# State-space rotations by ScalarE's sines, Toeplitz copies by parity, and MLP preloads moved later in a one-core decoder trunk

## The reference: what is computed

```python
dt = jnp.exp(log_step)[:, None]                      # 32 groups x 64 complex states
mag = jnp.exp(lam_re * dt); ang = lam_im * dt
abar_re, abar_im = mag * jnp.cos(ang), mag * jnp.sin(ang)
bb = coef * b                                        # complex, per group 64 x 16
bu = einsum('blgc,gpc->blgp', u, bb)
h[t] = abar * h[t-1] + bu[t]                         # associative scan over the tokens
y = einsum('gcp,blgp->blgc', c_re, h_re) - einsum(..., c_im, h_im) + d_skip * u
g = gelu(y); out = g * sigmoid(g @ w_glu)
```

## Time and profile before

| | us |
|---|---|
| runs | 2874.91, 2879.32, 2878.26 |
| median | 2878.26 |
| the profiled execution | 2878.83 |
| its span | 2877.1 |
| TensorE busy in it | 2715.2 (94%) |
| VectorE, GpSimd, ScalarE busy | 1487.3, 1051.8, 570.5 |

### The profile page before, as it was taken

How to read it: one execution, slowest core, us unless ns; L and a number is a source line. 1 busy time by engine, 2 the same in 40 slices (tenths; PEclk the granted TensorE clock), 3 DMA queues, 4 the chain that set the end, 5 groups by cost and what they waited for, 6 DMA issues and landing times.

```text
span 2877.1 us, 40626 instructions
## 1 busy us (share of the span) xinstructions
PE 2715.2 (94%) x16567; PEld 2580.3 (90%) x16567; DVE 1487.3 (52%) x1634; ACT 570.5 (20%) x880; POOL 1051.8 (37%) x414
## 2 busy tenths in 40 slices
PE   8979889989999999999999999977999999999997
PEld 6966579889999999999999999966989999999996
DVE  4983653714433444365667666665372344234437
ACT  4001542300000000034333443432130000000002
POOL 2532235476666666530000000010534444443542
PEclk9985799999999999999999999988999999999998
DMA  4332021352322222313111211202101111111111
GB/s 142 104 77 66 1 75 60 130 201 103 117 109 109 109 109 111 144 47 141 68 61 68 74 71 65 87 33 76 52 29 46 44 44 44 44 44 44 47 48 68
DMA packets 88993, 223.82 MB, mean 78 GB/s; under 512 B 22887, under 2 KB 38280, under 8 KB 88728
## 3 DMA queue, kind: packets, MB, share of 16 engines
q1 hardware_dynamic: 69280, 178.82, 17.8%
q10 hardware_dynamic: 19592, 43.32, 4.1%
HBM read 163.34 MB, written 58.74 MB: 77 GB/s over the span
## 4 chain that ended last, share of the span: by engine, by line
PE 63%; DVE 9%; ACT 3%; issue 2%; DMA 0%; POOL 0%; DVEq 0%; SPq 0%; ACTq 0%; POOLq 0%
PE ps L335 42%; PE ps L1708 6%; PE ps L1769 3%; PE ps L344 3%; DVE lev L1835 2%; ACT lev L1962 2%; DVE h_lo L695 2%; PE ps L415 2%; PE ps L448 1%; PE ps L462 1%; DVE ck L1835 1%; DVE ssq L673 1%; DVE cum L1835 1%; PE ps L1809 1%; DVE raw L1835 1%
## 5 line engine op out<-in xcount | busy, mean ns | idle before, releaser
L257 POOL TENSOR_TENSOR w_hi<-w_raw,ones 128x1024 fp32r<-128x1024 f32 x148 | 362.0, 2446 | 1603.1 <-PE ps L1708 653.4
L335 PE MATMUL ps<-a_hi,w_hi 128*128 128x352 f32 x1896 | 613.7, 324 | 11.7 <-POOL w_lo L259 9.3
L335 PE MATMUL ps<-a_hi,w_lo 128*128 128x352 f32 x1896 | 612.0, 323 | 0.0
L335 PE MATMUL ps<-a_lo,w_hi 128*128 128x352 f32 x1896 | 609.7, 322 | 0.0
L259 POOL TENSOR_TENSOR w_lo<-w_raw,w_hi 128x1024 fp32r<-128x1024 f32 x148 | 432.0, 2919 | 11.6
L335 PEld LDWEIGHTS ps<-a_hi,w_hi 128*128 128x128 f32 x1896 | 356.7, 188 | 13.7 <-POOL w_lo L259 5.8
L335 PEld LDWEIGHTS ps<-a_lo,w_hi 128*128 128x128 f32 x1896 | 358.6, 189 | 0.0
L335 PEld LDWEIGHTS ps<-a_hi,w_lo 128*128 128x128 f32 x1896 | 357.3, 188 | 0.0
L335 PE MATMUL ps<-h_hi,w_hi 128*128 128x352 f32 x1056 | 343.9, 326 | 6.1 <-POOL w_lo L259 6.0
L335 PE MATMUL ps<-h_hi,w_lo 128*128 128x352 f32 x1056 | 341.8, 324 | 0.0
L335 PE MATMUL ps<-h_lo,w_hi 128*128 128x352 f32 x1056 | 340.2, 322 | 0.0
(11 more groups left out here) (289 smaller groups left out, 4467.0 us busy)
## 6 DMA issues: line engine op xcount, KB each, us to landing
w_raw<-w SPq DMA_DIRECT2D x156, 512.0 KB, 3.5
p_raw<-w SPq DMA_DIRECT2D x32, 512.0 KB, 4.6
w_hi_scratch<-p_hi SPq DMA_DIRECT2D x32, 512.0 KB, 2.7
w_lo_scratch<-p_lo SPq DMA_DIRECT2D x32, 512.0 KB, 3.5
w_hi<-w_hi_scratch SPq DMA_DIRECT2D x32, 512.0 KB, 3.9
w_lo<-w_lo_scratch SPq DMA_DIRECT2D x32, 512.0 KB, 4.9
x_scratch<-x ACTq DMA_DIRECT2D x16, 528.0 KB, 2.9
x<-x_scratch ACTq DMA_DIRECT2D x16, 528.0 KB, 8.0
```

The source lines that it names most:

```text
L257: pool.tensor_tensor(hi, whole, bc(ones[:, 0:P], 1, KC), ALU.mult).then_inc(hi_made, 1)
L335: mm = pe.matmul(tiles[:, t], wt[:, b, w], at_[:, k, cols], start=(n == 0 and i == 0), stop=(n == len(ks) - 1 and i == 2))
```

## The change

1. **Rotations.** The doublings are replaced. VectorE multiplies the angle of one chunk by j (new input `jvec`, 0 to 127 on each partition, one more DMA that the first VectorE and ScalarE steps wait for), and folds the product into one turn by a rounding and a three-part subtraction. ScalarE makes sin(a/2), sin(a) and the square of the first (`act_rotations`, after `act_own_rows` and before `act_s5`); VectorE makes the cosine as 1 - 2 sin^2(a/2). Sine and cosine change places in `turn`.
2. **Toeplitz copies.** Each copy is cut in two by parity. SyncE issues all eight steps of parity 0, then steps 0 to 3 of parity 1; ScalarE issues steps 4 to 7 of parity 1. Parity 0 waits for one `lags_ready` only. The bytes are the same.
3. **Preloads.** The first MLP group has two preloads, after blocks 6 and 7; groups 1 to 6 have five each, after blocks 1, 2, 4, 5 and 7. The total stays 32.

```diff
-AHEAD_AFTER = {4: 2, 5: 2, 6: 2, 7: 2}
+AHEAD_AFTER = (1, 2, 4, 5, 7)
...
-            toep_rows(sp, range(4))
+            toep_rows(sp, 0, range(CH))
+            toep_rows(sp, 1, range(4))
             sp_k_outs(sp)
             sp_g(sp)
...
-            e = 0
             for j in range(8):
                 load(n0 + j, n0 + j, j % 2)
-                for _ in range(AHEAD_AFTER.get(j, 0)):
-                    if e == 0:
+                if j >= 6:
+                    if j == 6:
                         sp.wait_ge(x_parked, 16 * KC)
-                    ahead_in(e, e % 2)
-                    if e:
-                        ahead_out(e - 1, (e - 1) % 2)
-                    e += 1
-            with sp.Fori(1, GROUPS - 1) as g:
-                for j in range(8):
-                    load(g * 8 + (n0 + j), g * 8 + (n0 + j), j % 2)
-                    if j % 2:
-                        ahead_in(g * 4 + (4 + j // 2), (j // 2) % 2)
-                        ahead_out(g * 4 + (3 + j // 2), (j // 2 + 1) % 2)
+                    ahead_in(j - 6, j - 6)
+                    if j == 7:
+                        ahead_out(0, 0)
+            with sp.Fori(0, (GROUPS - 2) // 2) as pair:
+                e = 2
+                for half in range(2):
+                    for j in range(8):
+                        load(pair * 16 + (n0 + 8 + 8 * half + j), pair * 16 + (n0 + 8 + 8 * half + j), j % 2)
+                        if j in AHEAD_AFTER:
+                            ahead_in(pair * 10 + e, e % 2)
+                            ahead_out(pair * 10 + (e - 1), (e - 1) % 2)
+                            e += 1
...
+                        if name == "mlp0" and j >= 6:
+                            pool_ahead(pool, j - 6, j - 6, 16)
+                    if name == "mlp0":
+                        with pool.Fori(0, (GROUPS - 2) // 2) as pair:
+                            e = 2
+                            for half in range(2):
+                                for j in range(8):
+                                    block_of(pair * 2 + (1 + half), j)
+                                    if j in AHEAD_AFTER:
+                                        pool_ahead(pool, pair * 10 + e, e % 2, pair * 80 + 16 * (e // 2 + 1))
+                                        e += 1
...
-            while n < NCH:
-                wr, wi = bc(sm[:, 8], 2, n), bc(sm[:, 9], 2, n)
...
-                tt(new[0], old[0], wr, ALU.mult)
-                tt(tp, old[1], wi, ALU.mult)
-                tt(new[0], new[0], tp, ALU.subtract)
-                tt(new[1], old[0], wi, ALU.mult)
-                tt(tp, old[1], wr, ALU.mult)
-                tt(new[1], new[1], tp, ALU.add, prepared if 2 * n == NCH else None)
...
-                n *= 2
-                if n in (8, 32, 64):
-                    yield
+            half_turns, quotient = turn[:, 0], turn[:, 1]
+            tt(half_turns, bc(ang[:, CH], 2, NCH), bc(jvec[:], 1, GP), ALU.mult)
+            c.after(); c(TS(quotient, half_turns, 1 / (2 * math.pi), ROUND, ALU.mult, ALU.add))
+            c.after(); c(TS(quotient, quotient, -ROUND, None, ALU.add))
+            c.after(); c(STT(half_turns, quotient, -TWO_PI[0], half_turns, ALU.mult, ALU.add))
+            yield
+            for part in TWO_PI[1:]:
+                c.after(); c(STT(half_turns, quotient, -part, half_turns, ALU.mult, ALU.add))
+            c.after(); c(TS(half_turns, half_turns, PI_BELOW, -PI_BELOW, ALU.min, ALU.max), angles_ready)
+            yield
+            dve.wait_ge(turn_sines, 3)
+            c.after(); c(TS(turn[:, 1], turn[:, 1], -2.0, 1.0, ALU.mult, ALU.add), prepared)
...
+        def act_rotations(act):
+
+            act.wait_ge(angles_ready, 1)
+            act.activation(turn[:, 1], turn[:, 0], ACT.Sin, scale=0.5).then_inc(turn_sines, 1)
+            act.wait_ge(turn_sines, 1)
+            act.activation(turn[:, 0], turn[:, 0], ACT.Sin).then_inc(turn_sines, 1)
+            act.activation(turn[:, 1], turn[:, 1], ACT.Square).then_inc(turn_sines, 1)
...
-            pe.wait_ge(toep_in, 16 * CH)
+            pe.wait_ge(toep_in, 16 * 2 * CH)
...
-        def toep_rows(eng, steps):
+        def toep_rows(eng, par, steps):
             eng.wait_ge(toep_zero, 1)
-            eng.wait_ge(lags_ready, 2)
+            eng.wait_ge(lags_ready, par + 1)
             for s in steps:
-                eng.dma_start(toep[SC * s:SC * s + SC, :, :, SC * s:P], lags[:, :, :, 0:P - SC * s]).then_inc(toep_in, 16)
+                eng.dma_start(toep[SC * s:SC * s + SC, par, :, SC * s:P], lags[:, par, :, 0:P - SC * s]).then_inc(toep_in, 16)
```

More of the change, by code:

```diff
@@ L291, in last_group @@
                             block_of(GROUPS - 1, j, HID, spare(j - 6))
-                    e = 0
                     for j in range(8):
                         block_of(0, j, (-3, -2)[j] if j < 2 else None)
-                        for _ in range(AHEAD_AFTER.get(j, 0) if name == "mlp0" else 0):
-                            pool_ahead(pool, e, e % 2, 16 * (e // 2 + 1))
-                            e += 1
-                    with pool.Fori(1, GROUPS - 1) as g:
-                        for j in range(8):
-                            block_of(g, j)
-                            if name == "mlp0" and j % 2:
-                                pool_ahead(pool, g * 4 + (4 + j // 2), (j // 2) % 2, g * 32 + 16 * (3 + j // 4))
+                        if name == "mlp0" and j >= 6:
[9 more added lines that the diff above has]
+                                        e += 1
+                    else:
+                        with pool.Fori(1, GROUPS - 1) as g:
+                            for j in range(8):
+                                block_of(g, j)
                     last_group()
@@ L817, in build_trunk @@
         assert s1 + 9856 + 768 <= R1 + 118272
-        rest = at("rest", [P, GP * NCH // 2], s1 + 192)
-        assert 192 + GP * NCH * 2 <= 4288 + 192
+        jvec = at("jvec", [P, NCH], R1 + 116224)
         A0 = A_HI
@@ L877, in tt @@
                 c(TT_(out, a, b, op), signal)
-            dve.wait_ge(s5_in, 16 * 6)
+            dve.wait_ge(s5_in, 16 * 7)
             dve.wait_ge(dt_ready, 1)
@@ L1017, in act_prepare @@
         def act_prepare(act):
-            act.wait_ge(s5_in, 16 * 6)
+            act.wait_ge(s5_in, 16 * 7)
             act.activation(sm[:, 0], lam[:, 2], ACT.Exp).then_inc(dt_ready, 1)
@@ L1110, in quarter @@
                 i = slice(4 * q, 4 * q + 4)
-                wr, wi = turn[:, 0, i], turn[:, 1, i]
+                wr, wi = turn[:, 1, i], turn[:, 0, i]
                 vr, vi = (ps[:, 2 * (q % 2) + r].rearrange("p (i j) -> p i j", i=4) for r in range(2))
@@ L1166, in pool @@
                     i = slice(4 * q, 4 * q + 4)
-                    wr, wi, g = turn[:, 0, i], turn[:, 1, i], g_st[q % 2]
+                    wr, wi, g = turn[:, 1, i], turn[:, 0, i], g_st[q % 2]
                     hr, hi = (h_st[:, r, i, DB + 1:] for r in range(2))
@@ L1228, in act_s5 @@
                 act.activation(lags[:, par].rearrange("p (a b) n -> p a (b n)", a=4), ps[0:SC, 4:8], ACT.Copy).then_inc(lags_out, 1)
-            toep_rows(act, range(4, CH))
+            toep_rows(act, 1, range(4, CH))
             for g in range(TRIOS):
@@ L1241, in act_s5_loads @@
         def act_s5_loads(act):
-            for dst, name in ((lam, "s5_lam"), (b_in, "s5_b"), (c_in, "s5_c"), (kvec, "kvec"), (d_diag, "s5_d"), (h0, "s5_h0")):
+            for dst, name in ((lam, "s5_lam"), (b_in, "s5_b"), (c_in, "s5_c"), (kvec, "kvec"), (jvec, "jvec"), (d_diag, "s5_d"), (h0, "s5_h0")):
                 act.dma_start(dst[:], io[name]).then_inc(s5_in, 16)
@@ L2223, in _ @@
             act_own_rows(act)
+            act_rotations(act)
             act_s5(act)
@@ L2350, in layout @@
     o["kvec"] = np.broadcast_to(np.array(list(range(9)) + list(range(7, -1, -1)), np.float32), (P, 17)).copy()
+    o["jvec"] = np.broadcast_to(np.arange(SEQ // 8, dtype=np.float32), (P, SEQ // 8)).copy()
     o["ident"] = np.eye(P, dtype=np.float32)
```

15 lines of the change are left out of this document (1 added, 14 removed).

## The result

After: 2871.54 us, median of 13 runs (2858.28 to 2874.12), beside 2878.48 us for the kernel before in the same comparison (13 runs, 2874.91 to 2883.84). The ratio of the two kernels' runs is 0.9964, with a 95% interval of [0.995, 0.9977] (the two medians alone stand at 0.9976): faster, but by 0.36% where 0.6% was forecast, and outside the range of 2854 to 2868 us. Four of the 13 runs lie at 2858.28 to 2862.97, nine at 2869.83 to 2874.12. The profiled execution took 2874.12 us, with a span of 2872.3 us.

The account below looks back on a forecast made before the run. The kernel was taken as bound by a chain of waits from a weight block's DMA issued at 614.66 us. 2878.83 - 4.6 (parts 1 and 2) - 12.2 (part 3) = 2862.0, median 2861.4 us; range 2854 to 2868 us.

Parts of the forecast that it names:

- Part 1, transposes 2.5 us earlier: Rotations: v_t is evacuated earlier, so TensorE's transposes start at 166.7 instead of 169.2 us; bounds +1.8 and -5.
- the price of 0: ScalarE's rotations: Square after Sin taken to need no second table load, which would otherwise cost 1.28 us.
- Part 2, the wait for the landing turns into a wait for the states: Before the trios: earlier Toeplitz copies turn TensorE's 8 us wait for their landing into a wait for GpSimd's states.
- Parts 1 and 2, -4.6 us: Third trio, at 234.18 us before, starts at 229.5 or 230.0 us once its quarter of the states is ready.
- The trios at 0.50: TensorE's trios: idle time ahead keeps the granted clock at its lower level, the four remaining trios taking 39.0 us.
- Rival 3: The trios run at the full clock, ending 18.7 us sooner: 2843 us; chance 0.05.
- Part 3, -12.2 us: First MLP group: fewer preloads delay its weight blocks less; some 9 us are waits, the rest the clock they cost.
- Rival 4: Groups 1 to 6: the fifth preload holds up block 3; at 4 us per group 2885 us; chance 0.03.
- The later stages only move.: Whole kernel: a microsecond taken from TensorE's waits before 614.66 us comes off the end; later stages only shift.

Follow-up runs that it names:

- second profile: The changed kernel measured again, unchanged, against the kernel before: 2863.96 us, ratio 0.9931; its profile has the first lag stream at 7.16 us.
- both pauses filled: Changed kernel plus 20 unread identity matmuls on TensorE before its wait for the transposes and 8 before the lags: 2860.25 us, ratio 0.9925.
- The two later comparisons: The changed kernel measured twice more, unchanged, each against the kernel before: 2863.96 us (ratio 0.9931) and 2864.88 us (0.9941).
- reordered kernels: Changed kernel with the last rotation instruction behind v_t's evacuation and the in_ch copy: 2854.43 us; with identity matmuls before the lags 2853.23, in all pauses 2832.52.
- third profile of the changed kernel: The changed kernel measured a third time, unchanged, against the kernel before: 2864.88 us, ratio 0.9941; its profile has the first lag stream at 13.37 us.

## Why the prediction was wrong, by its own steps

- **Part 1, transposes 2.5 us earlier.** Right in direction and, in the profiles in which GpSimd's pass went first, close: 165.65 and 165.79 us against 166.7. In the others it was 163.5, by the race above, which the layout in time did not see: it took the last TENSOR_SCALAR as waiting for a GpSimd pass in any case. It also had the sines end at 163.7 us, and they ended at 160.93 us. The second table load did not come (Sin, Sin and Square took 1.92, 1.92 and 1.89 us with nothing between), so the price of 0 was right.
- **Part 2, the wait for the landing turns into a wait for the states.** Right: 0.91 us for the landing, 4.83 us for `h_st`.
- **Parts 1 and 2, -4.6 us: the step that failed.** "With the transposes 2.5 us earlier, that quarter is ready at 229.5 us" carried the lead through the lags unchanged. In the profile of the result the lag stream ran at the lower clock (13.44 for 7.16 us, and `quarter_in(0)` 3.68 for 1.97), and the mark came out at +0.96. In the same kernel's second profile the lags were fast and the mark was 228.34 us, -5.84, near the forecast 229.5. I had asked of the clock only what it does in the trios, not in the 1.97 us pause ahead of the lags, which stood in the same timeline as the earlier trace rows. What decides whether that pause costs the clock stays open; that it was the lag stream's time that ate the lead is what the profiles show. With both pauses filled the mark was 224.76.
- **The trios at 0.50.** Wrong for the first, which ran at 1.00 after its 0.91 us wait; right from the second on. It gained nothing, since the third waits for the states in either case (4.83 us). Rival 3, all trios at the full clock, came only where the waits were filled.
- **Part 3, -12.2 us.** Right in mechanism. In one pair of profiles -10.57, and nearly all of the missing 1.6 us lies in the first unit, part of it at the lower clock (15.40 for 13.85 us), which the prediction did not price; over all, the first group takes 97.3 to 101.3 us in the five profiles without part 3 and 84.4 to 86.9 in the thirteen with it, a mean of 99.5 against 86.0, -13.5. So the forecast lies between the two. Groups 1 to 6 did not grow: 93.4 to 94.6 us with four preloads and with five. Rival 4 fell.
- **"The later stages only move."** Not to the microsecond: what lies behind G took 4.46 us more in the profiled run with the same instructions, and between 2234.5 and 2244.3 us over the profiles (last section).
- The sum of 2862.0 against 2874.12 us is then: +5.6 (states, +0.96 for -4.6), +0.35 (attention), +1.6 (part 3 in this profile), +4.5 (the rest); 12.1 in all. The two later comparisons gave about the forecast change of -16.8 us (-20 and -17 by the ratios, -18 and -15 by the medians), the first did not. Run times alone can't tell whether the 13 runs there drew the slow lags more often, since the later stages scatter as much; their mean granted clocks lean to it, nine of 13.

## What to carry to other kernels

A gain in one engine's work is passed on in full only if TensorE's clock behind it stays as it was: list every pause of TensorE between the edit and the next bound, short ones too, and price the work behind each at both clocks. Look for a reorder that takes out or shortens a pause (here one instruction put behind the two that TensorE waits for, 2854 us instead of 2864 to 2872, with 1.35 us left of 4.8 to 7.2) before filling it, and fill only where no wait is added. Where two engines reach for the same moment within a few tenths of a microsecond, forecast two courses, and profile an unchanged kernel more than once before a few microseconds are explained.

## What the runs showed of the hardware

**Behind a pause of 2 us the clock may be halved for 14 to 17 us.** The same 1.97 us pause of TensorE ahead of the same 64 matmuls was followed by a stream of 7.16 us in six profiles and of 11.4 to 13.4 us in five, with the granted clock falling 0.5 to 2.6 us after work had resumed, in the middle of the busy stream. In the six profiles of the changed and reordered kernels in which fills stood in that pause, the stream took 7.16 us each time. That makes the pause the likely cause; which of its occurrences cost the clock is not settled.

**The same matmuls at the same granted clock have several paces.** VectorE's evacuations of MLP units mark 72 matmuls each. The third profile of the changed kernel, and then the first, in the second MLP:

```profile
2205.43 1.26 DVE L681 TENSOR_TENSOR ssq<-ps,rstd 128x1056 f32<-128x1056 f32 x1 [7.89 <-PE ps L343]
...
2216.87 1.26 DVE L681 TENSOR_TENSOR ssq<-ps,rstd 128x1056 f32<-128x1056 f32 x1 [4.21 <-PE ps L343]
```

```profile
2212.84 1.26 DVE L681 TENSOR_TENSOR ssq<-ps,rstd 128x1056 f32<-128x1056 f32 x1 [8.04 <-PE ps L343]
...
2224.44 1.26 DVE L681 TENSOR_TENSOR ssq<-ps,rstd 128x1056 f32<-128x1056 f32 x1 [4.37 <-PE ps L343]
```

11.44 against 11.60 us a unit, both at a granted clock of 1.00. In most groups of all profiles the units behind the group's start are at one of three values, 11.44, 11.52 or 11.60 us, mostly constant within the group and often another at the next one; whole groups take 93.4 to 94.6 us by it. Between the first and the third profile of the changed kernel the rest differs by 9.4 us (2244.1 and 2234.7), nearly what the change is worth in the first comparison. Of this 5.0 us lie in groups 1 to 6 of the first MLP (565.8 against 560.8 us) and 3.2 in the second, from its second group's first up unit to its last one (601.6 against 598.4). Why, these runs do not show.
